# Differential attention heads: the combination of the two maps leaves GpSimd, and the orders of the queues are changed around it

## The reference

```python
proj = u @ w_in                      # hc, bc, cc, q, k, v, gates
s1 = q1 @ k1.T * scale + bias        # bias = -slope * |qpos - kpos|
s2 = q2 @ k2.T * scale + bias
a = softmax(s1) - lam * softmax(s2)  # per head (4) and block of 128 queries (8)
o = rmsnorm(a @ v, subln_g) * (1 - lam_init)
g = sigmoid(gates + b_gate)          # merged = g0 * y_conv + g1 * y_attn
```

## Time and profile before

| | |
|---|---|
| median of 3 runs | 1368.92 us |
| profiled execution | 1368.93 us, span 1367.2 us |
| TensorE | busy 1352.3 us (99%) |
| VectorE | busy 949.5 us (69%) |
| ScalarE | busy 645.9 us (47%) |
| GpSimd | busy 182.7 us (13%) |
| granted TensorE clock | 0.999 of full speed |
| chain that ended last | 93% TensorE |

### The profile page before, as it was taken

The page is one execution under the profiler, slowest core; times in us unless marked ns, Lnnn a source line. Parts: engine busy times, 40 slices in busy tenths (PEclk is TensorE's granted clock), DMA queues, the critical chain, the costliest instruction groups (busy, mean ns, idle before and its releaser), DMA issues.

```text
span 1367.2 us, 17105 instructions
## 1 busy us (share of the span) xinstructions
PE 1352.3 (99%) x6305; PEld 1108.5 (81%) x6305; DVE 949.5 (69%) x1424; ACT 645.9 (47%) x992; POOL 182.7 (13%) x103
## 2 busy tenths in 40 slices
PE   9999999999999999999999999999999999999998
PEld 7777777777788888888888888888888888888886
DVE  7777778889667554667376886676764787665676
ACT  7677777785322344501243543333333444444453
POOL 0232323220000000000000333323333000000000
PEclk9999999999999999999999999999999999999999
DMA  5110101013221233455621355454445973335343
GB/s 189 32 31 17 31 17 31 17 39 100 62 63 33 91 121 111 141 154 168 238 85 63 117 168 162 146 163 143 150 162 209 368 250 112 100 124 193 110 129 108
DMA packets 141657, 162.19 MB, mean 119 GB/s; under 512 B 6861, under 2 KB 88970, under 8 KB 141450
## 3 DMA queue, kind: packets, MB, share of 16 engines
q1 hardware_dynamic: 135568, 148.27, 33.8%
q10 hardware_dynamic: 6010, 12.88, 2.4%
HBM read 114.98 MB, written 46.14 MB: 118 GB/s over the span
## 4 chain that ended last, share of the span: by engine, by line
PE 93%; ACT 3%; DVE 2%; issue 1%; DMA 1%; SPq 0%; ACTq 0%; DVEq 0%
PE psum L1093 36%; PE psum L927 23%; PE psum L1253 22%; PE psum L1054 3%; PE psum L1230 3%; PE psum L1007 3%; PE psum L974 2%; ACT e L1375 1%; DMA w_raw<-in_w_in 1%; PE psum L1202 1%; DVE act_lo L1864 0%; ACT at_hi L1388 0%; ACT L1399 0%; DVE v L2559 0%; ACT w_hi L1292 0%
## 5 line engine op out<-in xcount | busy, mean ns | idle before, releaser
L1253 PE MATMUL psum<-op 128*128 128x512 f32 x1344 | 305.0, 389 | 0.1
L1253 PEld LDWEIGHTS psum<-op 128*128 128x128 f32 x1344 | 252.2, 188 | 52.8 <-issue 0.5
L1725 ACT ACTIVATE op<-v 128x512 fp32r<-128x512 f32 x112 | 70.9, 633 | 152.1 <-PE psum L1253 148.3
L2438 DVE TENSOR_TENSOR op<-v,op 128x512 fp32r<-128x512 f32 x112 | 78.4, 700 | 89.6 <-ACT op L1725 89.6
L927 PE MATMUL psum<-act_hi,w_hi 128*128 128x512 f32 x256 | 103.2, 403 | 1.2 <-DVE act_lo L1864 1.2
L891 POOL TENSOR_TENSOR e<-e,e 128x1024 f32<-128x1024 f32 x31 | 74.6, 2406 | 222.3 <-ACT e L1382 222.3
L1093 PE MATMUL psum<-act_hi,w_hi 128*128 128x512 f32 x256 | 99.7, 389 | 0.9 <-ACT dev L1399 0.9
L927 PE MATMUL psum<-act_hi,w_lo 128*128 128x512 f32 x256 | 100.2, 391 | 0.0
L927 PE MATMUL psum<-act_lo,w_hi 128*128 128x512 f32 x256 | 100.0, 390 | 0.0
L1093 PE MATMUL psum<-act_hi,w_lo 128*128 128x512 f32 x256 | 99.6, 389 | 0.0
L1093 PE MATMUL psum<-act_lo,w_hi 128*128 128x512 f32 x256 | 99.6, 389 | 0.0
(11 more groups left out here) (272 smaller groups left out, 3089.4 us busy)
## 6 DMA issues: line engine op xcount, KB each, us to landing
f_raw<-f_scratch SPq DMA_DIRECT2D x112, 256.0 KB, 2.6
w_raw<-in_w_ff SPq DMA_DIRECT2D x32, 512.0 KB, 5.2
w_raw<-in_w_in SPq DMA_DIRECT2D x28, 512.0 KB, 5.0
f_scratch<-f_out SPq DMA_DIRECT2D x56, 256.0 KB, 2.3
v<-in_w_ff SPq DMA_DIRECT2D x12, 1024.0 KB, 7.0
gates_scratch<-staging ACTq DMA_DIRECT2D x32, 256.0 KB, 2.0
gate_in<-gates_scratch SPq DMA_DIRECT2D x16, 512.0 KB, 4.3
f_scratch<-staging SPq DMA_DIRECT2D x30, 256.0 KB, 2.1
```

What stands on the lines that cost most here:

```text
L1253: mm = nc.tensor.matmul(psum[:, (X_BANK, Z_BANK)[m % 2][t]], op[n % SLOTS][:, 2 + a, token_cols(t)], op[n % SLOTS][:, b], start=(m in (0, ...
L1725: nc.scalar.activation(op[n % SLOTS][:, 0], v_block[m][:, kt], ACT.Copy).then_inc(v_hi, 1)
L2438: vec.tensor_tensor(slot[:, 1], v_block[m][:, kt], slot[:, 0].bitcast(F32), ALU.subtract).then_inc(v_split, 1)
```

## The change

GpSimd's loop over the blocks goes. ScalarE scales map two by weight two in place of map one by its inverse, for all 32 blocks. VectorE no longer scales map two; in the next interval, after `maximum(i, n, 0)`, it forms map one times its inverse plus map two (`maps_summed`). The scaling stands before the turned map's high part in intervals 0, 2 and 6 and behind it in the others. The panel part of interval 3/4 moves to interval 5 on both engines, ahead of the exponentials on ScalarE and ahead of `weights` on VectorE. Head 3's third t sum moves from interval 5 to 4. In the first pair X2 stands ahead of Z1, and the logarithm, `x_copy(1)`, two `t_sum`/`g_part_lo` steps and the C22 sum take other places.

```diff
-    z_first: bool = False
...
-GATE = Pairs(0, ..., ("X2", "Z1", "X3", "Y", "X4", "Z2"), (0, 0), z_first=True)
+GATE = Pairs(0, ..., ("X2", "Z1", "X3", "Y", "X4", "Z2"), (0, 0))
...
-            for block in range(HEADS * QB - 1):
-                s = block % 2
-                pool.wait_ge(combine, 3 * block + 3)
-                pool.wait_ge(exp_done, 3 * block + 3)
-                nc.gpsimd.tensor_tensor(e[s][0][:], e[s][0][:], e[s][1][:], ALU.add).then_inc(a_ready, 1)
...
-            def first_scaled(i, n):
+            def second_scaled(i, n):
                 block = block_at(i, n)
                 s = block % 2
-                act.wait_ge(combine, 3 * block + 1)
-                nc.scalar.activation(e[s][0][:], e[s][0][:], ACT.Copy, scale=recip[s][:, 0:1]).then_inc(exp_done, 1)
+                act.wait_ge(combine, 2 * block + 2)
+                nc.scalar.activation(e[s][1][:], e[s][1][:], ACT.Copy, scale=weight2[s]).then_inc(exp_done, 1)
...
                 for n in range(QB):
-                    if n % 2 == 0 and n > 0:
-                        first_scaled(i, n - 1)
+                    if n in (2, 6):
+                        second_scaled(i, n - 1)
                     elif n == 0 and i > 0:
-                        first_scaled(i - 1, QB - 1)
+                        second_scaled(i - 1, QB - 1)
                     if n > 1:
                         turned_hi((i, "T", n - 2))
                     elif i > 0:
                         turned_hi((i - 1, "T", 6 + n))
-                    if n % 2 == 1:
-                        first_scaled(i, n - 1)
+                    if n % 2 == 1 or n == 4:
+                        second_scaled(i, n - 1)
...
+                    elif n == 5:
+                        panel_hi(HEAD_PANELS * (i + 1) + 1)
...
-                    if n in (1, 3, 5):
+                    if n in (1, 5):
                         panel_hi(HEAD_PANELS * (i + 1) + n // 2)
...
             last = HEADS - 1
+            second_scaled(last, QB - 1)
             turned_hi((last, "T", 6))
...
             copy_hi((HEADS, "g", 6))
+            o_logarithm(last, 1)
             t_hi_part(GATE, 1)
             for x in ("S2", "S3", "S1"):
                 g_part_hi(x, p)
-            o_logarithm(last, 1)
             t_hi_part(GATE, 2)
+            x_copy(GATE, 1, p)
             copy_hi((HEADS, "g", 7))
-            x_copy(GATE, 1, p)
...
                 vec.reciprocal(recip[s], exp_sum[s]).then_inc(combine, 1)
-                dve.wait_ge(combine, 3 * block + 1)
+                dve.wait_ge(combine, 2 * block + 1)
                 vec.tensor_scalar(weight2[s], recip[s][:, 1:2], neg_lam, None, ALU.mult).then_inc(combine, 1)
-                dve.wait_ge(combine, 3 * block + 2)
-                vec.tensor_scalar(e[s][1][:], e[s][1][:], weight2[s], None, ALU.mult).then_inc(combine, 1)
+
+            def maps_summed(i, n):
+                block = block_at(i, n)
+                s = block % 2
+                dve.wait_ge(exp_done, 3 * block + 3)
+                vec.scalar_tensor_tensor(out=e[s][0][:], in0=e[s][0][:], scalar=recip[s][:, 0:1], in1=e[s][1][:],
+                                         op0=ALU.mult, op1=ALU.add).then_inc(a_ready, 1)
...
                     maximum(i, n, 0)
+                    if n > 0:
+                        maps_summed(i, n - 1)
+                    elif i > 0:
+                        maps_summed(i - 1, QB - 1)
...
-                    elif n == 4:
+                    elif n == 5:
                         panel_lo(HEAD_PANELS * (i + 1) + 1)
...
-                    if i == HEADS - 1 and n in (1, 3, 5):
-                        t_sum(GATE, 3, n // 2)
+                    if i == HEADS - 1 and n in (1, 3, 4):
+                        t_sum(GATE, 3, (1, 3, 4).index(n))
...
             t_sum(GATE, 2, 1)
+            t_sum(GATE, 4, 0)
             t_lo(GATE, 1)
-            for x in ("S2", "S3", "S1"):
+            for x in ("S2", "S3"):
                 g_part_lo(x, p)
-            t_sum(GATE, 4, 0)
             t_lo(GATE, 2)
+            g_part_lo("S1", p)
             t_sum(GATE, 4, 1)
             g_sum("S4", p)
             g_part_lo("W11", p + 1)
             g_part_lo("S4", p)
             t_lo(GATE, 4)
+            gate_sum("C22", p)
```

More of the change, by code:

```diff
@@ L150 @@
     sums: tuple = ()
-    z_first: bool = False
     def __post_init__(self):
         self.order = pair_order(self.first, self.count, self.last_terms)
-        if self.z_first:
-            a, b = (self.order.index((x, self.first)) for x in ("X2", "Z1"))
-            self.order[a], self.order[b] = self.order[b], self.order[a]
         self.base = sum(self.earlier)
@@ L184, in t_hi_at @@
         return 4 + {3: 1, 2: 2, 4: 3, 1: 4}[n] if self.base else {3: 1, 1: 2, 2: 3, 4: 4}[n]
-GATE = Pairs(0, CONV_PAIRS + KT - GATE_PANELS // 2, ("X2", "Z1", "X3", "Y", "X4", "Z2"), (0, 0), z_first=True)
+GATE = Pairs(0, CONV_PAIRS + KT - GATE_PANELS // 2, ("X2", "Z1", "X3", "Y", "X4", "Z2"), (0, 0))
 FF1 = Pairs(PAIR0, NPAIR, ("X2", "Y", "X3", "Z1", "X4", "Z2"), (GATE.count // 2, GATE.count // 2))
@@ L2119, in head @@
                     maximum(i, n, 0)
+                    if n > 0:
+                        maps_summed(i, n - 1)
+                    elif i > 0:
+                        maps_summed(i - 1, QB - 1)
                     if n in (1, 5) and i > 0:
                         o_scale(i - 1, n // 4)
-                    elif n == 2:
+                    if n == 2:
                         if i > 0:
@@ L2143, in _ @@
             p, last = GATE.first, HEADS - 1
-            block = block_at(last, QB - 1)
-            maps, first = e[block % 2], recip[block % 2]
-            dve.wait_ge(combine, 3 * block + 3)
-            dve.wait_ge(a_ready, block)
-            vec.scalar_tensor_tensor(out=maps[0][:], in0=maps[0][:], scalar=first[:, 0:1], in1=maps[1][:], op0=ALU.mult,
-                                     op1=ALU.add).then_inc(a_ready, 1)
+            maps_summed(last, QB - 1)
             turned_lo((last, "T", 6))
@@ L2219, in _ @@
                 if p > GATE.first:
-                    gate_sum("C22", p - 1)
+                    if p > GATE.first + 1:
+                        gate_sum("C22", p - 1)
                     g_part_lo("S1", p)
```

## The result

The changed kernel takes 1371.69 us (median of 15 runs, 1371.58 to 1372.29), the kernel before 1368.93 beside it: 2.76 more, a ratio of 1.0020 with a 95% interval of 1.0013 to 1.0028. The forecast was 1372.3. The kernel is slower, but it passes the prediction's own bound for saying so (1371.66) by only 0.03. Two of the 15 executions of the kernel before took 7820 us, for a reason that no trace shows; they don't move its median.

A forecast was written before the change was run, and what follows sets the result against it. TensorE, busy 1352.3 of 1367.2 us, bounds the kernel, so only its gaps matter. New stalls with handoffs +9.47, old stalls -3.56, first pair -2.52 make +3.39: 1368.93 to 1372.3 us; 8-in-10 range 1368.8 to 1375.2.

The forecast's parts named there:

- the prediction's own bound: Whole kernel: a change is told from none from 0.2%, 2.7 us; above 1371.66 us it counts as slower.
- Mechanism: Heads: TensorE's old waits go, its turns wait about 11 times for VectorE's new sum; GpSimd 74.6 us less.
- the eleven places named: Interval 0 of heads 1-3, interval 4 of heads 1-3, interval 6 of heads 0-3, head 3's interval 2: 9.03 us.
- The slack of 0.86, or 0.25 with a copy: Heads' 8.14 us interval: turn possible after 7.28, or 7.89 with a q or k copy; high-part delay beyond the slack stalls.
- The handoff: Sum's end to TensorE's turn: 0.10 us taken, bounds 0.06 and 0.15; 0.44 more over 11 places.
- the old stalls: Heads 1 to 3, TensorE's waits for high part and scores' maximum: 3.56 us lost before, all to go.
- The first pair: Three gaps at the first pair (1.09, 0.89, 0.54 us) vanish through the new orders: 2.52 us gained.
- Rival B: Heads: the sum is never last to arrive, so no new stalls; faster, 1362.9 us; chance 0.15.
- Rival C: Heads' interval 6 comes out in time, taking 2.97 + 0.16 away; no change, 1369.2 us; chance 0.20.
- Rival D: First pair's gain doesn't come, second t's low part or S1 part being late; 1374.8 us; chance 0.15.
- The rule weighed: Interval 0, ScalarE's table load: skill's extra 1.38 us drain would cost 4 us more; prediction kept the rows' 1.88 us.

The follow-up runs named there:

- the kernel with 372 multiplies: Version with scaling behind the turned map and exponential ahead (1362.12), plus 372 20-column GpSimd multiplies in a new 80-byte-per-partition buffer: 1373.49 us, ratio 1.0034.
- the pair alone: The kernel before with only the first pair's new orders, heads old with GpSimd's adds: 1366.15 us, ratio 0.9979.

## Why the prediction held, step by step

**Mechanism.** Right. The waits moved from the high part and the scores to the new sum, at the eleven places named, with GpSimd 75 us lighter. Nine appear in the list; the two shortest (head 0's interval 6 and head 3's interval 4, 0.29 and 0.24) show only from turn to turn. One label is off: the old waits stand behind the turn of map 3, which by TensorE's order is interval 5, and not in the interval 4 where the new stall is. The sum isn't touched by it.

**The slack of 0.86, or 0.25 with a copy.** Right. Ordinary intervals stay at 8.14; each place that went over did so by the sum of its chain. The working used starts rather than ends, and it held to 0.04 in ten of eleven places. The exception is head 3's interval 6, 0.56 against 0.72: the third t sum held the low part back by 0.27 (it starts at 285.89, the turn of map 3 at 283.50, and 2.12 is the distance without it) where 0.35 was taken, 0.04 had gone into the longer interval 5 already, and the rest is hundredths.

**The handoff.** The size was nearly right and the cause was not. The sum's end to the turn is 0.06 in all three places shown, the least of the two bounds, where I took 0.10. What adds up instead is the restart: each interval that follows a stall takes 0.03 to 0.07 more, 0.57 in sum. The heads' total came out 0.10 above the prediction, and its parts partly cancel, which is luck: the stalls are 0.15 smaller, the restarts 0.13 larger than the handoffs that were put in for them, and the old stalls were 3.47 and not 3.56 (1.29 in head 2 where 1.33 was taken, 0.85 in head 3 where 0.9 was).

**The first pair.** Mis-sized by 0.30: 2.52 predicted, 2.82 measured with both halves present and 2.80 alone. A gap costs more than its idle time: the matmul after it starts late too. In the kernel before, the first matmul behind the first gap starts at 333.60 and the next one here:

```profile
333.90 0.39 PE L1093 MATMUL psum<-act_lo,w_hi 128*128 128x512 f32 x1
```

That is 0.31 (of the unrounded times) instead of 0.23. The other two gaps show the same, which makes 0.25, and a few steps of 0.23 to 0.24 behind the third bring the sum to 2.80. I had counted only from the last matmul before a gap to the first behind it.

**The end.** The prediction had nothing there; 0.51 came from the last stores, and 0.14 went beside the span. These net 0.37 and the pair's 0.30, less the heads' 0.10, are 0.57 of the 0.61 between 1372.3 and 1371.69; the rest is the medians' distance from the profiled executions. Two terms that were missing in the sum thus both made the kernel faster than forecast.

**Rival B**, the sum is never last: falsified. VectorE did not get faster without GpSimd. The maxima average 1220 ns after, 1.22 before; the panel's low part, which has two inputs in SBUF, averages 1218 in both kernels' heads. In the kernel with 372 multiplies, GpSimd was busy for 131 us beside the heads, and the grouped instructions of its VectorE (count, us busy, mean ns) read:

```profile
L1941 DVE CUSTOM_DVE_ANT_0 e<-psum,alibi 128x1024 f32<-128x1024 f32 x64 | 78.0, 1219 | 0.0
L1961 DVE SCALAR_TENSOR_TENSOR e<-e,small,e 128x1024 f32<-128x1024 f32 x32 | 40.8, 1276 | 2.6 <-ACT e L1380 2.6
```

Both are as with GpSimd idle (1220 and 1275). The Trainium skill (SBUF — State Buffer, Who interferes with whom) has a VectorE instruction with two SBUF inputs contend with GpSimd instructions that read SBUF; the sum is one, and these short multiplies did not lengthen it. Adds of the old size beside the new sum were not tried.

**Rival C**, interval 6 in time: falsified for this order, 0.29 to 0.98 were lost there. It comes in time when the scaling stands behind, as the version with that one edit shows. **Rival D**, the pair's gain doesn't come: falsified by the pair alone.

**The rule weighed.** The table load and the logarithm hold ScalarE for 100.26 - 98.38 = 1.88 again, and interval 0's stalls came to 0.91 to 0.94. The Trainium skill (ScalarE: Activation LUTs, What ACT_TABLE_LOAD costs) adds a drain of 1.38 us to the load, and by the prediction's working the stalls would then be 1.38 longer. The trace doesn't agree: there is no drain, as the rows of before already said.

## What to carry to other kernels

Find, in each interval, the instruction with which an engine's unbroken chain of work starts, and put nothing in front of it that is needed only later: moving one 1.04 us scaling behind it, and one high part behind an exponential, was worth 9.6 us here, while taking an engine out was worth nothing. Before an instruction is moved ahead of others, list who waits for those it passes, through every queue. And when an edit adds or resizes a buffer, compare the matmuls' pace in stages that it does not touch, product by product, before you explain the time by the edit.

## What the runs showed of the hardware

- **How the two operands of a matmul lie to each other sets its pace.** 4 more bytes per partition ahead of the later buffers: 48 matmuls of 128x512 in 11.20 us instead of 10.90, 1176 in 269.73 instead of 266.56, with nothing waiting. Products with one operand on either side of the new buffer take 233 to 234 ns instead of 227, those with both on one side 227 to 228. Which distances are slow was not tried beyond 4 and 80 bytes.
- **TensorE restarts slowly.** The second matmul behind a gap starts 0.31 us after the first instead of 0.23, a turn behind a stall takes 1.02 instead of 0.96 up to the scores, and removing three gaps of 2.52 in sum gave 2.82.
- **The last stores landed in 2.0 to 2.1 us** in the eleven kernels without GpSimd's adds in the heads, and in 2.5 and 2.6 in the three with them, 1000 us after the adds. Cause open.
- **Short GpSimd instructions beside VectorE** changed the means of VectorE's 1.2 us instructions by nothing: 1220 and 1219 ns, 1275 and 1276.
